# Levels brought forward, seven weight slots with an unrolled TensorE program, and a gather in two halves, in a three-mixer transformer kernel

## The reference, cut to what matters

```python
def _gla_scan(q, k, v, g, s0, with_outputs):      # once over the context, once over the latents, both directions
    ...                                           # s_new = exp(last) * s + (k * exp(last - cum))^T v
    scores = einsum('bhid,bhjd,bhijd->bhij', qc, kc, decay)     # decay = exp(cum_i - cum_j), j <= i
    o = einsum('bhid,bhde->bhie', qc * exp(cum), s) + einsum('bhij,bhje->bhie', scores, vc)

def _moe(h, w_router, b_router, w1, w3, w2):      # 16 experts, 2 for each of 256 tokens
    ...                                           # gates: 2 best experts of the best group of 4
    for e in range(N_EXPERTS):
        he = silu(h @ w1[e]) * (h @ w3[e])        # 1024 -> 512, twice
        out = out + gates[:, e:e + 1] * (he @ w2[e])            # 512 -> 1024
```

## Time and profile before

| | us |
|---|---|
| median of 3 runs | 1128.51 (1127.3 to 1128.78) |
| the profiled execution, whole | 1129.51 |
| its span, first to last instruction | 1127.7 |
| PE busy / DVE / ACT / POOL | 981.1 / 368.1 / 291.6 / 27.9 |
| mean granted TensorE clock | 0.958 of full speed |
| HBM traffic | 217.42 MB |

### The profile page before, as it was taken

How to read it: one execution, slowest core, us unless ns; L and a number is a source line. 1 busy time by engine, 2 the same in 40 slices (tenths; PEclk the granted TensorE clock), 3 DMA queues, 4 the chain that set the end, 5 groups by cost and what they waited for, 6 DMA issues and landing times.

```text
span 1127.7 us, 12169 instructions
## 1 busy us (share of the span) xinstructions
PE 981.1 (87%) x4326; PEld 513.3 (46%) x4327; DVE 368.1 (33%) x874; ACT 291.6 (26%) x674; POOL 27.9 (2%) x48
## 2 busy tenths in 40 slices
PE   3999979969867867787777999979899899997998
PEld 1463455536432222222222655547555444675763
DVE  1101572554251000000001313057676512345441
ACT  3200542332221000000001132156765501225330
POOL 0100200000001000000000000000000000000000
PEclk9999989989969999899898999989999999998999
DMA  9864563494295999969999211201645102442220
GB/s 354 297 222 150 102 222 112 151 358 163 98 349 189 397 397 396 396 242 399 397 394 364 92 56 66 70 5 40 243 167 145 43 0 75 150 149 75 75 76 37
DMA packets 99351, 217.42 MB, mean 193 GB/s; under 512 B 2852, under 2 KB 5208, under 8 KB 99176
## 3 DMA queue, kind: packets, MB, share of 16 engines
q1 hardware_dynamic: 94480, 206.45, 50.8%
q0 software_dynamic: 1696, 5.72, 2.1%
q10 hardware_dynamic: 3128, 4.62, 1.2%
HBM read 211.27 MB, written 5.51 MB: 192 GB/s over the span
## 4 chain that ended last, share of the span: by engine, by line
PE 70%; DMA 14%; DVE 6%; ACT 5%; issue 3%; SPq 1%; POOLq 1%; ACTq 0%; POOL 0%; DVEq 0%
PE bank L543 26%; DMA arena<-in_w_up_e_dram 10%; PE bank L555 9%; PE bank L759 9%; PE bank L830 4%; PE bank L913 3%; PE bank L511 3%; PE bank L932 3%; DMA arena<-in_w_mod_dram 3%; PE bank L923 2%; PE bank L772 2%; PE bank L747 1%; DMA arena<-in_mod_w_dram 1%; PE bank L825 1%; ACT arena L1165 1%
## 5 line engine op out<-in xcount | busy, mean ns | idle before, releaser
L543 PE MATMUL bank<-arena 128*128 128x512 f32 (+3 forms) x768 | 308.7, 560 | 6.3 <-ACT arena L1165 4.9
L543 PEld LDWEIGHTS bank<-arena 128*128 128x128 f32 x768 | 145.4, 192 | 157.9 <-issue 141.4
L759 PE MATMUL bank<-arena 128*64 128x512 f32 x544 | 136.3, 659 | 35.9 <-issue 30.7
L555 PE MATMUL bank<-arena 128*128 128x256 f32 (+1 forms) x384 | 99.5, 418 | 2.9 <-ACT arena L1513 1.5
L759 PEld LDWEIGHTS bank<-arena 128*64 128x64 f32 x544 | 43.9, 150 | 127.7 <-issue 120.8
L555 PEld LDWEIGHTS bank<-arena 128*128 128x128 f32 x384 | 72.6, 191 | 31.3 <-issue 21.7
L772 PE MATMUL bank<-arena 128*64 128x512 f32 x272 | 62.1, 597 | 9.6 <-ACT arena L1352 9.0
L1350 ACT ACTIVATE arena<-bank 128x256 f32<-128x256 f32 x16 | 6.1, 383 | 217.6 <-PE bank L759 217.6
L511 PE MATMUL bank<-arena,silu_c 128*32 128x512 f32 x384 | 51.1, 658 | 12.3 <-DMA arena<-in_mod_w_dram 9.3
L1945 DVE TENSOR_TENSOR arena<-arena,bank 128x256 f32<-128x256 f32 x16 | 6.7, 422 | 154.9 <-ACT arena L1350 154.9
L913 PE MATMUL bank<-arena 64*128 64x512 f32 (+3 forms) x160 | 49.4, 571 | 4.5 <-ACT arena L1610 2.3
(11 more groups left out here) (325 smaller groups left out, 952.6 us busy)
## 6 DMA issues: line engine op xcount, KB each, us to landing
arena<-in_w_down_e_dram SPq DMA_DIRECT2D x16, 2048.0 KB, 19.9
arena<-in_w_gate_e_dram SPq DMA_DIRECT2D x16, 2048.0 KB, 17.0
arena<-in_w_up_e_dram SPq DMA_DIRECT2D x16, 2048.0 KB, 21.4
arena<-in_w_mod_dram SPq DMA_DIRECT2D x12, 2048.0 KB, 10.6
arena<-in_mod_w_dram SPq DMA_DIRECT2D x12, 2048.0 KB, 8.2
arena<-in_gla_w_in_dram SPq DMA_DIRECT2D x6, 2048.0 KB, 11.1
arena<-in_cd_w_in_dram SPq DMA_DIRECT2D x6, 2048.0 KB, 7.7
arena<-in_ab_w_in_dram SPq DMA_DIRECT2D x5, 2048.0 KB, 9.5
```

The lines of the kernel that those rows point to most:

```text
L543: mm = pe.matmul(ps[:, 0:n], lhs[:, k, tile * P:(tile + 1) * P], w[:, k, c0:c0 + n], start=(k == 0), stop=(k == kd_ - 1))
L555: mm = pe.matmul(ps[:, i * n:(i + 1) * n], w[:, k, c * P:(c + 1) * P], rhs[:, k, 0:n], start=(k == 0), stop=(k == KC - 1))
L759: mm = pe.matmul(up_b[64 * j:64 * j + 64, :], h[:, k, :], w13[:, :, k, 256 * j:256 * j + 256], start=(k == 0), stop=(k == KC - 1), tile_po ...
```

## The change

One: PE does `level(0)` directly after the equal blocks; `v1_0`, `v1_1` and the states move between the levels, the r projections and modulation columns shift back with them, ACT copies `mod(9)` before the turned keys, and the front loads change slots. Two: a seventh slot (6) lies low in the arena, the experts' matrices go round through the slots 6, 3, 4, 5, 1, 2, 0, SP's and PE's programs are written out over 16 experts, and the first `ab` loads are asked for in another order. Three: the gather is done in two halves of 256 columns, and POOL stages expert 0 after the first. Several small tiles move in the arena to make room. The core of the diff:

```diff
-        SCAN_FILL = [[("r", 0)], [("r", 1), ("mod", 10)], [("r", 2)], [("r", 3), ("mod", 11)], [("mod", 12)],
-                     [("mod", 13)], [("mod", 14)], [("mod", 15)]]
+        SCAN_FILL = [[("v1", 0)], [("v1", 1), ("mod", 10)], [("state", 0)], [("r", 0)], [("r", 1), ("mod", 11)],
+                     [("r", 2), ("mod", 12)], [("r", 3), ("mod", 13)], [("mod", 14), ("mod", 15)]]
...
-                       (10, 0), ("r1", 1), (11, 2), (12, 0), (13, 2), (15, 1), (14, 0), ("o0", 2), ("o1", 0), (16, 1),
+                       (10, 0), ("r1", 1), (11, 0), (12, 2), (13, 0), (14, 2), (15, 1), ("o0", 0), ("o1", 2), (16, 1),
                        (17, 4)]
...
+        CYCLE = [6, 3, 4, 5, 1, 2, 0]
+        expert_slot = {}
+        for e in range(NE):
+            g, u, d = (CYCLE[(3 * e + j) % 7] for j in range(3))
+            if slot_at(g) > slot_at(u):
+                g, u = u, g
+            expert_slot[e] = (g, u, d)
...
-            for k in range(KC):
-                name = f"gath{k}"
-                ps = banks.open(pe, name, (hg_a, hg_v)[k % 2], k // 2 + 1)
-                for t in range(TT):
-                    mm = pe.matmul(ps[:, :], xn2[:, t, k * P:(k + 1) * P], sel[:, t, :],
+            for part in range(2):
+                for k in range(KC):
+                    name = f"gath{part}{k}"
+                    ps = banks.open(pe, name, (hg_a, hg_v)[k % 2], 4 * part + k // 2 + 1)
+                    for t in range(TT):
+                        mm = pe.matmul(ps[:, 0:T], xn2[:, t, k * P:(k + 1) * P], sel[:, t, T * part:T * part + T],
...
-                        mm = pe.matmul(up_b[64 * j:64 * j + 64, :], h[:, k, :], w13[:, :, k, 256 * j:256 * j + 256],
+                        mm = pe.matmul(up_b[64 * j:64 * j + 64, :], h[:, k, :], blocks[:, g + n:u + n + 1:u - g, :],
...
-            with pe.Fori(0, NE // 2) as i:
-                for b in range(2):
-                    e = i * 2 + b
+            for e in range(NE):
+                for j in range(2):
+                    landed_expert(e, j)
+                any_extra = pe.value_load(flags[:, e * EXTRA:e * EXTRA + 1], min_val=0, max_val=1)
+                with pe.If(any_extra > 0):
...
+                pe.wait_ge(hs_ready, e + 1)
+                up(hs[e % 2], e, up_done)
+                pe.wait_ge(ff_ready, e + 1)
+                turn_ff(ff_turned)
+                landed_expert(e, 2)
+                pe.wait_ge(ffT_ready, e + 1)
+                down(e, down_done)
...
+            for e in range(NE):
+                js = (0, 1, 2) if expert_slot[e][0] == CYCLE[3 * e % 7] else (1, 0, 2)
+                for j in js:
+                    s = expert_slot[e][j]
+                    if s in last_in:
+                        e0, j0 = last_in[s]
+                        sp.wait_ge(down_done if j0 == 2 else up_done, e0 + 1)
+                    elif s == 6:
+                        sp.wait_ge(o_ready, TT)
+                    elif s == 3:
+                        banks.wait(sp, "y11")
+                        sp.wait_ge(y_added, 4)
+                    elif s == 4:
+                        banks.wait(sp, "row17")
+                    fill_expert(e, j)
+                    last_in[s] = (e, j)
+            sp.wait_ge(down_done, NE - 2)
...
                 if ld[0] == "ab3c":
+                    sp.wait_ge(up_done, NE)
+                if ld[0] == "ab2":
                     sp.wait_ge(down_done, NE)
...
             level_exp(0)
+            mod(9)
             for g in range(4):
...
             level_exp(1)
-            mod(9)
...
             stage(0, 0)
+            pool.wait_ge(hg_a, KC)
+            pool.wait_ge(hg_v, KC)
             stage(1, 1)
```

More of the change, by code:

```diff
@@ L207, in build @@
         RING = MAIN + 3 * SLOT
+        SPARE = KC * (2 * T + CAP)
+        blocks = arena[:, :].rearrange("p (n c) -> p n c", c=256)
         def view(off, *dims):
@@ L676, in _ @@
                         project(f"r{n // TT}_{n % TT}", f"r{n // TT}", 0, 512, n % TT, hT, r_copied, n + 1)
+                    elif what == "v1":
+                        project(f"v1_{n}", "v1", 0, 512, n, hT, v1_ready, V1_AT[n])
+                    elif what == "state":
+                        states()
                     else:
@@ L1241, in _ @@
             level_exp(1)
-            mod(9)
-            for g in range(4):
-                ps = banks.wait(act, f"state{g}")
-                act.activation(S_sb[:, 2 * g:2 * g + 2, :], ps[:, :].rearrange("p (a d) -> p a d", a=2), ACT.Copy)\
-                   .then_inc(state_ready, 1)
-            v1_copy(0)
-            v1_copy(1)
             for li in range(len(LEVELS)):
@@ L1265, in _ @@
                            .then_inc(r_copied, 1)
+                    elif what == "v1":
+                        v1_copy(n)
+                    elif what == "state":
+                        for g in range(4):
+                            ps = banks.wait(act, f"state{g}")
+                            act.activation(S_sb[:, 2 * g:2 * g + 2, :], ps[:, :].rearrange("p (a d) -> p a d", a=2),
+                                           ACT.Copy).then_inc(state_ready, 1)
                     else:
@@ L1302, in _ @@
             norm(2, xn_ctx, lambda t: None, False)
-            for k in range(0, KC, 2):
-                ps = banks.wait(act, f"gath{k}")
-                act.activation(hg[:, k, 0:2 * T], ps[:, :], ACT.Identity,
-                               bias=coef[:, 2, 1, k:k + 1], scale=coef[:, 2, 0, k:k + 1]).then_inc(hg_a, 1)
+            for part in range(2):
+                for k in range(0, KC, 2):
+                    ps = banks.wait(act, f"gath{part}{k}")
+                    act.activation(hg[:, k, T * part:T * part + T], ps[:, 0:T], ACT.Identity,
+                                   bias=coef[:, 2, 1, k:k + 1], scale=coef[:, 2, 0, k:k + 1]).then_inc(hg_a, 1)
             act.preload_act_table(ACT.Silu)
@@ L1911, in _ @@
                 link(dve.tensor_reduce(gates_ab[:, :, j], tmp32, AX.X, ALU.add))
[L1912 to L1915 removed]
+            for part in range(2):
+                for k in range(1, KC, 2):
+                    ps = banks.wait(dve, f"gath{part}{k}")
+                    dve.tensor_scalar(hg[:, k, T * part:T * part + T], ps[:, 0:T], coef[:, 2, 0, k:k + 1],
+                                      coef[:, 2, 1, k:k + 1], ALU.mult, ALU.add).then_inc(hg_v, 1)
             norm_rows(2, xn_ctx)
```

171 lines of the change are left out of this document (71 added, 100 removed).

## The result

The changed kernel takes 1099.17 us, the median of 4 runs (1095.78 to 1102.54); before, in the same comparison, it was 1128.61. The ratio is 0.9742, with a 95% interval of 0.971 to 0.9773. The profiled execution took 1099.73 us.

What follows compares the result with a forecast made beforehand. PE was taken as the bound, with holes, and DMA as the bound between experts. Gains of 16.2 + 2.3 + 5.5 + 5.5 = 29.5 us take the profiled 1129.51 to 1100.0, median 1099.0; range 1090 to 1108.

Steps and rivals of the forecast that it cites:

- Case (a): Whole kernel: the forecast itself comes true, 1091 to 1107 us; chance 76%.
- The levels, 16.2: Scan stage: 17.9 us of idle and slow time go, less 1.5 for a new wait and 0.2 for signals.
- the wait at `mod(15)`: Scan stage: its load to slot 1 lands at 234.7, PE is there at 233.3; a new wait of about 1.5 us.
- the slow records: Scan stage: state products lose 2.2 us (9.23 against 7.03) and `mod(14)` 1.7 (3.64 against 1.92); both could go.
- just in time: Scan stage: DVE's multiplications for `level(0)` are done at 157.04, so PE starts it at 157.4 without waiting.
- rival (b): Scan stage: DVE's and ACT's 8.4 us round per level shows through; gain falls by 7 to 14, 1106 to 1113; 9%.
- The gather, 2.3: Before the experts: PE's 2.69 us wait for POOL vanishes, the halved gather grows 0.4; net 2.3 us, bounds 0 and 2.7.
- The slots, 5.5 + 5.5: Expert loads: one transfer less behind the first pause, 5.5 us; pause at expert 8 5.5 us shorter, 5.0 left.
- Rival (c): Expert loads: slots give less, expert 8's pause stays whole; 1104.5, or 1110 if the seventh slot does nothing; 8%.
- The unrolling, 0: Expert bodies on PE: some 14 x 200 more instructions, ten packets, cost 0 because PE waits 4.0 us per expert for DMA.
- Rival (d): Expert bodies: unrolled PE stalls at each skip; slower from 4.0 us per body, at 5.4 us 1151; 4%.
- Everything behind the experts, 0: From expert 15's `up` to the end: the rest of the kernel stays as long as before, moving with the experts.

Runs made afterwards that it cites:

- the part alone: The kernel before with only the new order of levels, values and states, new front slots and ACT's earlier copy: 1113.34 us, ratio 0.9861.
- the six dead copies: The changed kernel plus six never-run copies of `up` (384 PE instructions) per expert behind a branch on a flag read at run time: 1195.86 us, ratio 1.0593.
- its repeat: The changed kernel with six `up` copies behind a constant branch, which can't have been in the program, so it serves as a repeat: 1098.21 us, ratio 0.9711.

## Why the prediction was right, step by step

The forecast was 1099.0 with a range of 1090 to 1108 and 0.94 for faster; measured were 1099.17 and faster. Case (a) holds, by the mechanism forecast: the stops of the scan stage, the wait for POOL and the pauses of the loads shrank, and each part alone gave its share. Its exactness is partly luck: the terms that were too small sum to 3.3 us, and 3.1 went the other way.

**The levels, 16.2.** Measured 15.9 in the changed kernel's trace and 15.7 by the time of the part alone. The first output was forecast for 237.2 and came at 237.48; the wait at `mod(15)` was forecast as 1.5 and is 1.52; the slow records came back to full speed as said (7.07 and 1.92). One step was wrong: `level(0)` was to start right at 157.4, "just in time", but PE waited 1.49 us for DVE's second multiplication and started at 157.95. It costs 0.6 us against the forecast start, since PE's equal blocks were done at 156.46, earlier than in the kernel before. That is one of the signs that the prediction had named against itself, a wait for DVE's second multiplication, but at the first level alone, and it was under 1.5 us in every kernel with the new order. The later levels never wait for DVE, so rival (b) is out.

**The gather, 2.3.** It was mis-sized by the 0.4 us of growth: 64 records took 15.47 to 16.57 us in eleven kernels with the halves, 15.88 in the middle one, around the 15.92 of before. The wait for POOL vanished in every kernel with the halves (for the one bracket that still names POOL, see the six dead copies above). From the gather's start to `up` the changed kernel takes 3.2 us less, 2.7 of the wait and 0.45 of a gather that ran short.

**The slots, 5.5 + 5.5.** The first term stood. The second was too small: the second pause is 2.4 us and not 5.0. The step that was off took away exactly one transfer, 5.5, from the 10.5 of before. What it left out is that the pause ends when expert 8's main `up` ends, and that the way there got shorter. From the extra `up` to the main one it takes 459.59 - 444.32 = 15.3 us instead of 17.1, since the extra `up` took 7.09 and not 8.78; and POOL's queue held it up by 1.69 and not 2.48. These are 1.7 and 0.8, 2.5 us together, of the 2.6 that are missing. The speed of the extra `up` goes with the stop ahead of it: 7.09 us behind stops of 1.69 and 1.28 (the changed kernel and its repeat), 8.46 to 8.78 behind stops of 2.41 to 4.14 in the five kernels with six slots and a whole extra body. Why the stop got shorter with seven slots wasn't tried; 0.7 of the 0.8 us lie between the end of POOL's staging and PE's start (0.75 us before, 0.05 after). To better than 1 us this account isn't closed, for with six slots and the unrolled program the pause was 9.3 and not 10.5. Rival (c), slots that give less, is out: a kernel with six slots is 12.4 us slower on this distance.

**The unrolling, 0.** Measured 0 to 1 us of gain. Twelve more packets were fetched, against ten forecast, fourteen of them between 320 and 570 (the DMA queues of the kernel after in that stretch):

```profile
q8 instruction: 14, 0.23, 0.4%
```

Where loads didn't hold it up, PE went through the unrolled bodies at 12.53 us. Rival (d) did not come about, but its 4% weren't for nothing: the dead copies brought such stops. It was priced at 5.4 us from a store under the same load, and with 384 dead instructions in a body most stops are 4.6 to 5.4 us, with three of 10.1 to 11.1, about twice that. The size came near, though nothing shows that a stop and a store have the same cause. What was missing in its argument is the length: an extra body of about 100 instructions leaves the program at an estimated 0.8 packets per body, where no stop shows; at 1.1 the distance over the experts grew by 4.5 us, at 1.6 by 31.

**Everything behind the experts, 0.** It took 2.8 us longer. The same steps at the start of the attention stage, as stretches (columns as above) of the kernel after and then of the kernel before:

```profile
720.70:727.70 7.00, 6.99 (x24) 5.31 (x25) 5.95 (x11) 3.51 (x9) 0.00 (x0) 0.61 0.00 1
...
763.00:767.50 4.50, 4.50 (x16) 3.40 (x16) 2.54 (x9) 2.19 (x9) 0.00 (x0) 0.62 0.58 213
```

```profile
753.60:759.60 6.00, 5.95 (x25) 4.75 (x26) 4.96 (x10) 3.50 (x9) 0.00 (x0) 0.74 0.00 0
...
794.80:797.80 3.00, 3.00 (x18) 2.26 (x18) 2.16 (x8) 1.99 (x9) 0.00 (x0) 1.00 0.90 328
```

The idle time ahead of each is the same in both (5.76 and 5.77 us, then 2.22 and 2.22), and the work is the same; the granted clock is not: 0.61 against 0.74, and 0.62 against 1.00, so part of each stretch ran at the 1.2 GHz level. The two stretches are 1.0 and 1.5 us longer, 2.5 of the 2.8 us. With six slots this distance was 532.1 to 532.5 in five profiled executions and 534.9 in a sixth. With seven it was 530.9, 531.9, 532.9, 533.3, 534.7, 534.9, 535.4 and 537.8, all with the changed kernel's program behind the experts. So the change doesn't always bring the loss (530.9 is the shortest of all); whether it makes it likelier stays open.

## What to carry to other kernels

Where loads set the pace, a slot more was worth about one transfer for each pause in the stream of loads (5.5 and 6.9 us at 5.5 for a transfer), not a share of the whole: find the pauses in the table of stretches, multiply each by its missing rate, and ask what keeps the last slot busy. Splitting a matrix into two loads with a semaphore each removed the rest of the second pause and 3.3 us of the first, for no memory.

Unrolling a loop that jumps over rare code was free here at 0.8 packets of the instruction queue per body of 12.5 us, dead code included, nearly free at 1.1 (4.5 us over 16 bodies) and dear at 1.6 and 2.4; count the packets per body before adding a second rare branch. And distances between the same steps of two traces settle questions of 2 us that the whole times, with 3.5 us between two comparisons of one kernel, can't.

## What the runs showed of the hardware

Dead instructions on PE are not free even when they are never run. 192 in a body of 12.5 us cost 25 us in all, 384 cost 97, in stops of mostly 4.4 to 5.4 us that the waits put down to issue, and most of them are followed by slow products. The instruction queue's packets grow with them (42, 47, 55 and 67), though none of them runs.

The front of the kernel wanders. With the same program up to there, the first output came at 251.68 to 256.19 in three profiled executions without the change of the levels, and at 235.00 to 238.24 in eleven with it, so one trace alone places a stage only to about 3 us.
